# A decoder layer's prologue in four stages of two contraction tiles, with the conditioning sums mostly on VectorE

## The reference, cut to what matters

```python
def reference(x, c, ..., w_ada, b_ada, g_pre_mix, w_in, ...):     # x (1, 1024, 1024), c (1, 1024)
    ada = (c @ w_ada + b_ada).reshape(B, 6, D)                    # w_ada (1024, 6144)
    shift_m, scale_m, gate_m = ada[:, 0], ada[:, 1], ada[:, 2]
    h = rms_norm(x, g_pre_mix) * (1.0 + scale_m) + shift_m
    proj = h @ w_in                                               # (1024, 1024) @ (1024, IN_W)
    qa, ka, va, qb, kb, vb, f_logit, gate_logit = split(proj)
    ...                                                           # rotary, two attentions, gates, FFN
```

## Time and profile before

| | |
|---|---|
| median of 3 runs | 1428.35 us (1427.76 to 1429.79) |
| the profiled execution | 1428.78 us, its span 1427.0 us |
| PE busy | 1396.8 us (98%) |
| DVE, ACT, POOL busy | 987.4, 552.0, 576.3 us |
| chain that ended last | PE 90%, DVE 5%, ACT 2%, DMA 1% |

### The profile page before, as it was taken

The page is one execution under the profiler, slowest core; times in us unless marked ns, Lnnn a source line. Parts: engine busy times, 40 slices in busy tenths (PEclk is TensorE's granted clock), DMA queues, the critical chain, the costliest instruction groups (busy, mean ns, idle before and its releaser), DMA issues.

```text
span 1427.0 us, 19793 instructions
## 1 busy us (share of the span) xinstructions
PE 1396.8 (98%) x6914; PEld 1145.4 (80%) x6922; DVE 987.4 (69%) x1412; ACT 552.0 (39%) x1120; POOL 576.3 (40%) x463
## 2 busy tenths in 40 slices
PE   5999999999999999999999999999999999999998
PEld 2998787777777888888888888888888888888886
DVE  4876798565554666776744896677667766697767
ACT  3711487555552000010433543333333333464443
POOL 1215755233254444433302247776777774100000
PEclk9999999999999999999999999999999999999999
DMA  9500022111322645343342244444334446876773
GB/s 348 156 16 18 22 86 56 50 63 38 111 75 81 173 123 147 107 119 114 104 148 74 74 136 133 144 147 143 124 123 124 130 135 222 304 234 202 249 236 118
DMA packets 174811, 185.69 MB, mean 130 GB/s; under 512 B 15904, under 2 KB 128648, under 8 KB 174096
## 3 DMA queue, kind: packets, MB, share of 16 engines
q1 hardware_dynamic: 168336, 178.87, 40.1%
q10 hardware_dynamic: 6400, 5.83, 1.2%
HBM read 148.98 MB, written 35.69 MB: 129 GB/s over the span
## 4 chain that ended last, share of the span: by engine, by line
PE 90%; DVE 5%; ACT 2%; DMA 1%; issue 1%; SPq 1%; DVEq 0%; ACTq 0%
PE PS L1973 69%; PE PS L2113 10%; PE PS L2167 2%; PE PS L2194 2%; PE PS L2221 2%; PE PS L2222 2%; DMA wada<-in_w_ada_dram 1%; PE PS L2150 1%; PE PS L2186 1%; DVE htmp L1384 1%; DVE act_lo L1388 1%; DVE ada_acc L1367 1%; DVE rope_b L1440 1%; PE PS L1986 1%; SPq L560 1%
## 5 line engine op out<-in xcount | busy, mean ns | idle before, releaser
L920 POOL TENSOR_TENSOR ws_lo<-s_tmp,ws_hi 128x512 fp32r<-128x512 f32 x76 | 117.7, 1549 | 84.0 <-ACT ws_hi L1217 84.0
L1528 DVE TENSOR_TENSOR pt_lo<-PS,pt_hi 128x512 fp32r<-128x512 f32 (+3 forms) x128 | 74.0, 580 | 75.9 <-ACT pt_hi L1053 75.5
L1973 PE MATMUL PS<-T_hi,ws_hi 128*128 128x512 f32 x320 | 124.5, 389 | 0.0
L1973 PE MATMUL PS<-T_lo,ws_hi 128*128 128x512 f32 x320 | 124.5, 389 | 0.0
L1973 PE MATMUL PS<-T_hi,ws_lo 128*128 128x512 f32 x320 | 124.5, 389 | 0.0
L1973 PE MATMUL PS<-db_hi,da_hi 128*128 128x512 f32 x308 | 119.8, 389 | 0.0
L1973 PE MATMUL PS<-db_lo,da_hi 128*128 128x512 f32 x308 | 119.8, 389 | 0.0
L1973 PE MATMUL PS<-db_hi,da_lo 128*128 128x512 f32 x308 | 119.8, 389 | 0.0
L829 POOL CAST w_hi<-wraw 128x1024 fp32r<-128x1024 f32 x39 | 42.0, 1078 | 187.2 <-PE PS L1973 111.9
L1973 PE MATMUL PS<-act_hi,w_hi 128*128 128x512 f32 x288 | 113.3, 393 | 0.0
L1973 PE MATMUL PS<-act_hi,w_lo 128*128 128x512 f32 x288 | 112.1, 389 | 0.0
(11 more groups left out here) (331 smaller groups left out, 3707.2 us busy)
## 6 DMA issues: line engine op xcount, KB each, us to landing
dn_raw<-ff_dram SPq DMA_DIRECT2D x66, 256.0 KB, 4.2
adaraw<-in_w_ada_dram SPq DMA_DIRECT2D x32, 512.0 KB, 4.2
wraw<-in_w_in_dram SPq DMA_DIRECT2D x25, 512.0 KB
wraw<-in_w_ffn_in_dram SPq DMA_DIRECT2D x24, 512.0 KB, 5.0
ff_dram<-sl SPq DMA_DIRECT2D x22, 512.0 KB, 5.9
w2t<-in_w_ffn_out_dram SPq DMA_DIRECT2D x22, 512.0 KB, 6.7
w2sum_dram<-w2s SPq DMA_DIRECT2D x11, 1024.0 KB, 5.8
dn_raw<-w2sum_dram SPq DMA_DIRECT2D x44, 256.0 KB, 4.2
```

Source lines behind the costliest of these rows:

```text
L920: pool.tensor_tensor(ws_hl[i][1][:, :, :], left(par, i), ws_hl[i][0][:, :, :].bitcast(F32), ALU.subtract)\
L1528: nc.vector.tensor_tensor(pt_hl[gp % 3][1][:, 0:n], PS[:, 4 + gp % 2, 0:n], pt_hl[gp % 3][0][:, 0:n].bitcast(F32), ALU.subtract).then_inc( ...
L1973: ins = nc.tensor.matmul(out_ap, lhs[a], rhs[b], start=first and i == 0, stop=last and i == 2)
```

## The change

The prologue is done in four stages `s` = 0 to 3. Stage `s` loads 256 shift and 256 scale columns of `w_ada` (those of the contraction tiles 2s and 2s+1), as two pieces of four row blocks, each piece two transfers of 512 KB with 1 KB runs, and behind them the values' weights of the tiles 2s and 2s+1. Its sums are made by TensorE for row blocks 0 and 1 (`ADA_PE` = 2, `ada_row`) and by VectorE for blocks 2 to 7. ScalarE copies the row, TensorE turns both to four columns, VectorE takes them (`ada_take`), and `h` of the tiles 2s and 2s+1 follows. ScalarE now evaluates each tile of `h` twice, rounded (`act_hi`) and full (`h_full`), and VectorE's low part is one subtraction of the two, both in SBUF. GpSimd makes the high and the low part of all eight tiles of the values' weights. The squares of the second half's row tiles move ahead of the first values' copies, `values(2)` ahead of the transposes 8 to 11, and the norms' scaling is split two and two between ScalarE and VectorE in both halves. What follows `project(1)` is unchanged but for the numbers of semaphores.

```diff
-    ADA_ORDER = (0, 2, 1, 3)
-    ADA_DVE = ((0, 0, 4), (2, 0, 4), (1, 0, 6), (3, 0, KD))
+    ADA_PE = 2
+    ADA_PIECES = ((0, 4), (4, KD))
+    N_STAGE = 4
...
@@ sync
+            for s in range(N_STAGE):
+                load_stage(s)
+                load_wv(2 * s)
+                load_wv(2 * s + 1)
...
-            sp.wait_ge(wv_split, KD - len(WV_DVE))
-            sp.wait_ge(wv_split_d, len(WV_DVE))
+            sp.wait_ge(wv_split, KD)
...
@@ gpsimd
             for k in range(KD):
-                if k in WV_DVE:
-                    continue
+                pool.wait_ge(tile_in[k], 32)
+                pool.tensor_copy(wv_hl[0][:, k], wvraw[:, k]).then_inc(wv_hi_ok, 1)
                 pool.wait_ge(wv_hi_ok, k + 1)
                 pool.tensor_tensor(wv_hl[1][:, k], wvraw[:, k], wv_hl[0][:, k].bitcast(F32), ALU.subtract)
...
@@ scalar
+            for s in range(N_STAGE):
+                act.wait_ge(row_ready, s + 1)
+                nc.scalar.activation(adarow[:, s % 2], PS[0:1, 2], ACT.Copy).then_inc(row_ok, 1)
+                act.wait_ge(ada_taken, s + 1)
+                for k in (2 * s, 2 * s + 1):
+                    h_hi_part(k, a_mix, adac)
+            for t in (4, 5, 6):
+                square(t)
             v_hi_part(0)
             v_hi_part(1)
...
@@ vector
+            ada_part(0, 0)
+            ada_part(0, 1)
+            for s in range(N_STAGE):
+                ada_take(s)
+                h_lo_part(2 * s)
+                if s + 1 < N_STAGE:
+                    ada_part(s + 1, 0)
+                h_lo_part(2 * s + 1)
+                if s + 1 < N_STAGE:
+                    ada_part(s + 1, 1)
...
-                nc.vector.tensor_scalar(tmp[:, g % 2], act_hl[0][...].bitcast(F32), shift[:, k:k + 1], None, ALU.subtract)
-                nc.vector.scalar_tensor_tensor(out=act_hl[1][:, k, cols], in0=PS[:, h_bank(g)], scalar=scale[:, k:k + 1],
-                                               in1=tmp[:, g % 2], op0=ALU.mult, op1=ALU.subtract).then_inc(h_lo, 1)
+                nc.vector.tensor_tensor(act_hl[1][:, k, cols], h_full[:, g % 2], act_hl[0][:, k, cols].bitcast(F32), ALU.subtract)
...
@@ tensor
+            for s in range(N_STAGE):
+                if s + 1 < N_STAGE:
+                    ada_row(s + 1)
+                first_values(2 * s)
+                if s + 1 < N_STAGE:
+                    transpose_group(2 * s + 2, xin[:, 0:4])
+                    ada_columns(s + 1)
+                    ada_rest(s + 1)
+                first_values(2 * s + 1)
+                if s + 1 < N_STAGE:
+                    transpose_group(2 * s + 3, xin[:, 0:4])
+            values(2)
+            pe.wait_ge(xn_ok, N_XN)
+            for g in range(KD, KD + 4):
+                transpose_group(g, xin[:, 4:8])
+            values(3)
```

More of the change, by code:

```diff
@@ L133, in hybrid_layer @@
     CS = 72 * KB + 8 * KD * WV
-    wada = at("wada", H0, [P, 4, KD, NT])
-    ada_acc = at("ada_acc", R0 + CS + 8 * KB, [P, 2, NT])
+    QW = 2 * P
+    wada_s01 = at("wada_s01", R0, [P, 2, KD, 2 * QW])
+    wada_s23 = [at(f"wada_s{2 + i}", H0 + i * 32 * KB, [P, KD, S]) for i in range(2)]
+    wada = [wada_s01[:, 0], wada_s01[:, 1], wada_s23[0][:, :, NT:S], wada_s23[1][:, :, NT:S]]
+    ada_acc = at("ada_acc", R0 + CS, [P, 2, 2 * QW])
+    adarow = at("adarow", R0 + 33 * KB, [1, 2, 2 * QW])
     posi = at("posi", R0 + CS + 4 * KB, [P, S], I32)
@@ L958, in norm_rows @@
                 act.wait_ge(rstd_ok, half + 1)
-                for t in range(4 * half, 4 * half + (2 if half else 4)):
+                for t in (4 * half, 4 * half + 1):
                     ins = nc.scalar.activation(xin[:, t], xin[:, t], ACT.Copy, scale=rstd[:, t:t + 1])
@@ L1366, in _, with ada_part @@
+            def ada_part(s, i):
+                acc = ada_acc[:, s % 2]
+                k0, k1 = ADA_PIECES[i]
+                dve.wait_ge(ada_in[s][i], 32)
+                for k in range(max(k0, ADA_PE), k1):
+                    if k == ADA_PE:
+                        ins = nc.vector.tensor_scalar(acc, wada[s][:, k], pcols[:, k:k + 1], None, ALU.mult)
                     else:
-                        ins = nc.vector.scalar_tensor_tensor(out=acc, in0=wada[:, j, k], scalar=pcols[:, k:k + 1], in1=acc,
+                        ins = nc.vector.scalar_tensor_tensor(out=acc, in0=wada[s][:, k], scalar=pcols[:, k:k + 1], in1=acc,
@@ L1991, in _ @@
             nc.tensor.transpose(PS[:, 5, 0:88], prow[:, :], ident[0:88, 0:88]).then_inc(prow_ready, 1)
-            def ada_row(nth):
-                j, _, k0 = ADA_DVE[nth]
-                pe.wait_ge(ada_in[j][1], 16)
-                for k in range(k0, KD):
-                    nc.tensor.matmul(PS[0:1, ROW_BANK[nth]], pcols[:, k:k + 1], wada[:, j, k], start=(k == k0), stop=False)
-            def ada_rest(nth):
-                pe.wait_ge(acc_ready, nth + 1)
-                nc.tensor.matmul(PS[0:1, ROW_BANK[nth]], ones[:, 0:1], ada_acc[:, nth % 2], start=False, stop=True).then_inc(row_ready, 1)
@@ L2012, in ada_columns @@
                 for oc in range(4):
-                    ins = nc.tensor.matmul(PS[:, 4, 4 * j + oc:4 * j + oc + 1], ada_acc[:, nth % 2, oc * P:(oc + 1) * P],
-                                           ones[:, 0:1], start=False, stop=last and oc == 3)
+                    c0 = 4 * s + oc
+                    ins = nc.tensor.matmul(PS[:, 3, c0:c0 + 1], ada_acc[:, s % 2, oc * P:(oc + 1) * P], ones[:, 0:1],
+                                           start=False, stop=oc == 3)
                 ins.then_inc(ada_used, 1)
```

257 lines of the change are left out of this document (111 added, 146 removed).

## The result

| | before | after |
|---|---|---|
| median | 1428.49 us (1427.76 to 1429.79, 4 runs) | 1451.23 us (1449.93 to 1451.69, 4 runs) |
| ratio of after to before | | 1.0158 (95% interval 1.0146 to 1.0170) |
| profiled execution | 1428.78 us, span 1427.0 | 1451.26 us, span 1449.5 |
| first matmul of `project(0)` | 73.88 | 96.88 |

The change makes the kernel 22.7 us slower; the forecast was 11.6 (1440.0) with a range to 1446. The time stands where the prediction looked for it. So the whole difference lies ahead of `project(0)`, and the room for VectorE's sines, which the prediction put at nothing, did cost nothing.

What follows compares the result with a forecast made beforehand. The start of TensorE's unbroken work at `project(0)` was taken to bound the kernel: 0.6 us later from circles and tail plus 11.3 of GpSimd contention, 11.9 in all, giving 1440.3 (1440 in round), range 1431 to 1446.

Steps and rivals of the forecast that it cites:

- the room for VectorE's sines: Behind `project(0)`'s start: sine tables begin some 4 us later against it, about 1 us of room left; counted nothing, 1 to 2 us if it fails.
- the start of `project(0)` decides: TensorE runs without a gap from `project(0)`, at 73.88 before; what moves that start is the gain or loss.
- The loads and where they land: Prologue loads: 1 KB runs at about 350 GB/s, first values' weights near 19, the last near 42.5.
- The circle of 8.64 us: One stage, from one taking of columns to the next: columns 1.50, ScalarE's first tile 1.48, VectorE 5.66 us.
- a start at 74.5 with no contention: `project(0)` after three circles and the tail, without GpSimd's interference: 0.6 us later than before.
- GpSimd's work holds up VectorE: In the stages, GpSimd's casts and subtractions block VectorE through shared ports: 11.3 us, bounds 0 and 16.5; chance 73%.
- the 11.3 of 1.7, 3.3, 3.5 and 2.8: Contention of GpSimd with VectorE in us, for stages 0, 1, 2 and 3 in turn.
- The term of the units: Stage 3: the projection units' weights land at 53, GpSimd's cast and subtraction meet VectorE's last additions, +2.8 us.
- the sentence on the low clock: In the stages with contention, TensorE waits 3 us or more each, which covers the loss from its low clock.
- the 0.6 of the sum: `project(0)` without contention starts at 74.5, 0.6 us later than before, by the summed circles and tail.
- a chance only as what sets the time alone: Low clock rival: each stage's TensorE burst could begin at the low level, 1.7 us longer; 1434, chance 7%.
- Its price without contention, 5.4 us: Low clock on TensorE with 0.1 us to spare in a circle: three circles and the tail give +5.4, 1434.

Runs made afterwards that it cites:

- the last two kernels: Changed kernel, values' weights cast on ScalarE and subtracted in VectorE's waits, units late, transposes first: 1432.15 us; same with VectorE's next-stage operations ahead, two transposes inside `values(3)`: 1430.29 us.
- the last one: Kernel with subtractions in VectorE's waits, plus VectorE's first two next-stage operations moved ahead and transposes 12 and 13 inside `values(3)`: 1430.29 us.

## Why the prediction was half right

**By its steps.** That the start of `project(0)` decides: right, to under 1 us in every run. The loads and where they land: right (354 against 350 GB/s; 42.21 against 42.5). The circle of 8.64 us and a start at 74.5 with no contention: right once the two disturbances are gone (8.7 to 8.8 us, 75.29), in the shortest of nine executions; the median one is 2.0 us longer. That GpSimd's work holds up VectorE: right, and nearly right in size. The excess over quiet operations in the trace after is 1.5 us in stage 0 (4.62 against 3.12), 3.7 in stage 1 (from 27.02 to 35.73, 8.71 us, against 5.02 for the same seven operations with GpSimd idle), 2.9 in stage 2 and 4.6 in stage 3: 12.6 against the 11.3 of 1.7, 3.3, 3.5 and 2.8. The term of the units was the mis-sized one, 2.8 forecast and 4.6 found: I had let one unit's cast and subtraction meet VectorE, and both units' did.

**The step that failed** is the sentence on the low clock: with contention "TensorE waits 3 us or more a stage and the loss is covered". The waits are 1.6 to 3.7 us, 2.4 in the mean, and they do not cover it, for two reasons. The columns come after the wait: eight tiny matmuls at the low level, 1.96 us from sum to taking in place of 1.15, in three of four stages, 2.9 us together with the 0.46 of stage 1. And the transposes of the second tile stand behind twelve value matmuls, so that what these lose at the low level (1.7 us by the prediction's figure) reaches ScalarE and VectorE: 1.9 us in stage 2, 2.6 in the tail (3.15 against 0.58), and from `values(2)` to `project(0)` it is 1.5 us longer (20.6 us; 19.1 with GpSimd idle and the transposes first). That is 8.9 us; with the 12.6 of contention and the 0.6 of the sum it makes 22.1 of the 23.0 us by which `project(0)` is late.

Moving the transposes alone gave 9.0 us at `project(0)` in the profiled executions (8.3 by the medians): 4.5 from the two waits for the second tile, 1.3 from columns, two of which are back at 1.15, 1.5 behind `values(2)`, and 1.5 of contention, since VectorE's operations then met GpSimd's less (11.1 us over their quiet times, not 12.6). A third way in which the low clock costs shows where little else is left, in the last two kernels: TensorE's own work fills a circle of 8.6 to 8.9 us at the full clock, and where the clock falls the circle is 10.2 us.

The prediction had read the very stretch in which TensorE ran at 0.57, and priced it at 1.7 us a stage; it then compared this with TensorE's idle time and not with what stands behind TensorE. I had given the clock a chance only as what sets the time alone; that it could come on top of contention stood beside it without a price. Its price without contention, 5.4 us, was short too: by its own terms, three times 1.6 and a tail of 1.7, it is 6.5, and the kernel with GpSimd idle in the stages measured 8.0. The Trainium skill, "TensorE: Matmul & The Clock Gate", HAM oscillation, warns of loops of short bursts with waits for data between; the trace agrees, with 0.50 to 0.52 in three stretches behind such waits, which here are for VectorE's sums and not for loads.

**The sum, from the medians.** 1428.4 to 1431.65 with GpSimd idle and the transposes first: 3.2 us, the circle and the tail (the prediction had 0.6; in the one profiled execution of that kernel it is 1.4). To 1443.0 with GpSimd at work: 11.3, mostly the contention (in the profiled executions 12.6, of which 11.1 are in VectorE's operations and 1.5 in late columns); that it is the forecast's very figure is chance. To 1451.2 with the transposes behind: 8.3, mostly the low clock by way of the order. Taken in the other order the parts are 4.8 for the transposes with GpSimd idle and 14.8 for GpSimd with the transposes behind, so 3.5 us belong to both: that fits with longer waits for VectorE making the clock fall more often, which was not tried by itself.

**What stays open.** What exactly makes the clock fall was not isolated. In the kernel after it fell behind waits of 1.6 to 3.7 us with tiny matmuls around them, and with GpSimd idle and the transposes first it stayed up for 20 us in which TensorE never waited; but it also fell with no wait before it: near 42 in the kernel with eight added matmuls, near 40 in the last one, and near 49.5 in that same kernel with GpSimd idle and the transposes first. Each time it was a little behind the small matmuls of the columns, which it had come through unchanged in other stages of the same trace. That the low clock makes up the rest between 1429.64 and the median 1431.65 is likely, but no trace of a longer execution of that kernel shows it.

## What to carry over

Time that an engine waits covers its own slowness only if the slow work stands ahead of the wait; ask what follows the wait and who is released by it. When TensorE works in bursts between waits, put the small work that releases other engines (here four transposes) ahead of the large work that nobody waits for, and price it at the low clock. Work of a helper engine that holds up the engine of the critical circle is better done in that circle's own waits: the same subtractions cost 6 us more on GpSimd (1438.5) than in VectorE's own waits (1432.15), part of it by way of TensorE's clock.

## What the runs showed of the hardware

A VectorE operation that meets a subtraction of GpSimd's lasts as if it waited for the whole of it: in the kernel after, three of them, one low part at 43.19, one at 53.68 and the addition at 57.39, end 0.54 to 0.55 us after GpSimd's subtraction does. Four additions beside the values' weights take 4.62 to 4.76 us there and in the kernel with the added matmuls, in place of 3.11, longer by about one subtraction of GpSimd's (1.55 to 1.87 us), though a cast lies beside them as well; beside the units' splits, in the kernel with the added matmuls, the same four took 8.48. I had not expected that it reaches tiny operations: the 128x2 operation behind a taking took 0.89 us in place of 0.16 in the kernel with the transposes first, when GpSimd was at work. GpSimd loses less: its casts are 1.17 to 1.24 us beside VectorE and 0.72 alone, its subtractions 1.87 and 1.55. And TensorE, at work for 19.97 of 20 us, kept its full clock there although a third of its matmuls are one to four columns wide (18 of some 54 in a circle); it lost it 1.5 us later, without a wait.
